# Six projection tiles of the mixing layer fed with the scaled raw stream instead of its normed form

## The reference, cut to what matters

```python
def first_block(x, c, positions, ...):
    cond = jax.nn.silu(c)
    mod = cond @ w_ada[l] + b_ada[l]
    sh1, sc1, gt1, sh2, sc2, gt2, sh3, sc3, gt3 = split(mod, 9)
    u = modulate(rmsnorm(h, g_norm_ffn1[l]), sh1, sc1)
    h = h + 0.5 * gt1 * swiglu(u, w_ffn1_in[l], w_ffn1_out[l])
    u = modulate(rmsnorm(h, g_norm_mix[l]), sh2, sc2)
    h = h + gt2 * token_mixing(u, cos, sin, w_in[l], ...)
    ...
```

## Time and profile before

| | us |
|---|---|
| median of three executions | 2532.84 (2530.0 to 2533.72) |
| the profiled execution | 2532.03 |
| its span in the trace | 2530.2 |
| TensorE busy in it | 2445.1 (97%) |
| VectorE busy in it | 1801.1 (71%) |
| ScalarE busy in it | 1106.5 (44%) |
| bytes read from memory | 451.09 MB, 179 GB/s over the span |

### The profile page before, as it was taken

The page is one execution under the profiler, slowest core; times in us unless marked ns, Lnnn a source line. Parts: engine busy times, 40 slices in busy tenths (PEclk is TensorE's granted clock), DMA queues, the critical chain, the costliest instruction groups (busy, mean ns, idle before and its releaser), DMA issues.

```text
span 2530.2 us, 39280 instructions
## 1 busy us (share of the span) xinstructions
PE 2445.1 (97%) x15654; PEld 2226.9 (88%) x15654; DVE 1801.1 (71%) x3467; ACT 1106.5 (44%) x1656; POOL 0.2 (0%) x4
## 2 busy tenths in 40 slices
PE   4998999999999999999999999999999999998998
PEld 3998989999999888788888998888998888988997
DVE  7888887788977446768877669897785344676555
ACT  3444565544463324724223662232562222566443
POOL 0000000000000000000000000000000000000000
PEclk8999999999999999999999999999999999999999
DMA  8997656769855431653543256676374333122653
GB/s 317 334 332 266 211 193 191 250 234 313 304 196 188 140 100 59 208 159 125 154 141 121 85 183 202 192 237 199 119 241 148 94 125 95 62 92 91 202 185 99
DMA packets 161671, 454.72 MB, mean 180 GB/s; under 512 B 17745, under 2 KB 21329, under 8 KB 161489
## 3 DMA queue, kind: packets, MB, share of 16 engines
q1 hardware_dynamic: 161488, 452.21, 54.3%
HBM read 451.09 MB, written 1.05 MB: 179 GB/s over the span
## 4 chain that ended last, share of the span: by engine, by line
PE 77%; DVE 4%; ACT 4%; issue 1%; DMA 0%; ACTq 0%; DVEq 0%; SPq 0%
PE PS L1297 24%; PE PS L1299 24%; PE PS L1298 24%; DVE own L1803 1%; PE PS L1457 1%; PE PS L1324 1%; PE PS L1322 1%; ACT own L1525 1%; ACT Uh L1588 1%; PE PS L1506 1%; ACT NT L1592 1%; DVE X L1784 1%; PE PS L1489 0%; DVE X L1899 0%; ACT spare L1525 0%
## 5 line engine op out<-in xcount | busy, mean ns | idle before, releaser
L1297 PE MATMUL PS<-Uh,own 128*128 128x256 f32 (+1 forms) x2080 | 655.1, 315 | 30.4 <-DVE Ul L1888 21.7
L1298 PE MATMUL PS<-Ul,own 128*128 128x256 f32 (+1 forms) x2080 | 646.6, 311 | 0.0
L1299 PE MATMUL PS<-Uh,own 128*128 128x256 f32 (+1 forms) x2080 | 646.4, 311 | 0.0
L1525 ACT ACTIVATE own<-raw 128x1024 fp32r<-128x1024 f32 x425 | 443.3, 1054 | 360.9 <-PE PS L1299 298.6
L1803 DVE TENSOR_TENSOR own<-raw,own 128x1024 fp32r<-128x1024 f32 x425 | 515.0, 1220 | 76.6 <-ACT own L1525 76.2
L1297 PEld LDWEIGHTS PS<-Uh,own 128*128 128x128 f32 x2080 | 401.5, 193 | 55.4 <-issue 29.5
L1298 PEld LDWEIGHTS PS<-Ul,own 128*128 128x128 f32 x2080 | 401.8, 193 | 19.8 <-issue 0.2
L1299 PEld LDWEIGHTS PS<-Uh,own 128*128 128x128 f32 x2080 | 401.6, 193 | 19.7
L1297 PE MATMUL PS<-Hh,own 128*128 128x256 f32 (+1 forms) x1088 | 345.2, 317 | 0.0
L1298 PE MATMUL PS<-Hl,own 128*128 128x256 f32 (+1 forms) x1088 | 340.9, 313 | 0.0
L1299 PE MATMUL PS<-Hh,own 128*128 128x256 f32 (+1 forms) x1088 | 340.9, 313 | 0.0
...
## 6 DMA issues: line engine op xcount, KB each, us to landing
...
```

The source lines that it names most:

```text
L1297: e.matmul(o, ll, rh, start=start, stop=False, skip_group_check=shared)
L1298: e.matmul(o, lh, rl, start=False, stop=False, skip_group_check=shared)
L1299: return e.matmul(o, lh, rh, start=False, stop=stop, skip_group_check=shared)
L1525: e.activation(parts(w.n)[0], raw[:, w.n % RING, :], ACT.Copy).then_inc(s["whi"].tell(w.n), 1)
```

## The change: raw operands, and sums between them

For six tiles TensorE no longer waits for the norm. The token's reciprocal is a factor per token and the shift adds a constant per output feature, so both can be applied behind the product. ScalarE and VectorE write high and low parts of `X` times gain into the columns 256 to 511 of `Uh` and `Ul` ("rawhi", "rawlo"); the shift stands in two further columns, for which the rows of both tiles grow from 512 to 528 words (`UW`). The matmuls of these tiles have 258 columns. The first stops after six rows for the sums of squares, then goes on. VectorE multiplies each result by the reciprocal, copies the product with the shift to `lift`, and ScalarE adds it. The normed rows are still made, for the tiles from the seventh on. The first four rows' squares are folded on VectorE, not the first six. Two places in `spare` are opened in the first layer, so that two more chunks are split ahead; the queries that are written over them wait for those chunks' products. The rates of mods change: 1.7 in place of 1.5 in the first layer and 0 in its last slab, 0.6 in the remaining projections (0.9 before), 0.9 for values and attention (0.9, then 0.6), 1.5 for the gates (0.9), 1.6 in the second feed-forward layer (1.4). `T2`, a tile of the second block's mixing, moves onto the first 128 columns of the bias tile in `GW`.

```diff
+UW = 528
+RAW = 6
+RAW_FOLDED = 4
...
@@ class Plan
-        if len(t["todo"]) > BEHIND:
+        if sums and len(t["todo"]) > BEHIND:
             self.sums(t)
...
+            self.raw_lows()
             for k in (mm,) if alone else (mm - 1, mm):
-                self.square(self.tallies[LAT], k)
+                self.square(self.tallies[LAT], k, RAW_FOLDED if raw else FOLDED, not raw)
+                if raw:
+                    self.put("rawhi", st=raw, k=k, after=(st, at, k, 0))
+                    self.raws.append((raw, k))
...
@@ schedule
-    p.rate = 1.5
-    main = p.ffn("w1", "w1o", LAT, [(("w1", 0), "half", 0, 2)], False)
+    p.rate = 1.7
+
+    def before_raw():
+        p.column(("nm", "c"), "gm", 0, 4)
+        p.mod_until(0, 3)
+        p.put("rawshift", q=0, f=3)
+        p.rate = 0.0
+
+    main = p.ffn("w1", "w1o", LAT, [(("w1", 0), "half", 0, 2)], False, then={len(SLABS) - 1: before_raw}, raw="nm")
...
+    for at in (0, 1):
+        p.open(at, "modded", (31, 0))
...
-    p.rate = 0.9
-    first = p.rms("nm", 0, 3, "gm", (0, 0), w1_last, 0, ("wpqk", [("wpqk", t_) for t_ in range(3)]))
...
+    p.clear = [c for at in (0, 1) for c, _, _ in p.close(at)]
+    t = p.tallies.pop(LAT)
+    raw = [p.raw_tile("wpqk", 0, 0, 6)]
+    p.raw_lows()
+    while t["todo"]:
+        p.sums(t)
+    raw[0] = p.raw_tile("wpqk", 0, 6, KT, raw[0].n, raw[0].bank)
+    p.put("stat", n=t["n"], r=LAT, bank=t["bank"], eps=1e-6)
+    raw.append(p.raw_tile("wpqk", 1, 0, KT))
+    p.put("root", n=t["n"], r=LAT)
...
+    for k in range(0, KT, 2):
+        for kk in (k, k + 1):
+            p.put("rms", st="nm", k=kk, n=t["n"], r=LAT, after=w1_last, q=0, f=3)
+        if len(made) < RAW:
+            made.append(p.raw_tile("wpqk", len(made), 0, KT))
+        raise_one()
...
+    p.rate = 0.6
...
+    p.rate = 0.9
...
-    p.rate = 0.9
+    p.rate = 1.5
...
-    p.rate, p.mod_limit = 1.4, EARLY_PAIRED * 16
+    p.rate, p.mod_limit = 1.6, EARLY_PAIRED * 16
...
@@ build
-        Uh = sb("Uh", [P, KT, 512], F32R)
-        Ul = sb("Ul", [P, KT, 512], F32R)
+        Uh = sb("Uh", [P, KT, UW], F32R)
+        Ul = sb("Ul", [P, KT, UW], F32R)
...
@@ TensorE
+                elif w.what == "rawmm":
+                    on.wait_ge(s["wlo"], w.n)
+                    if w.k == 0:
+                        claim(w.bank)
+                    for k in range(w.k, w.f):
+                        on.wait_ge(s["raw_lo"], k)
+                        m = three(PS[:, w.bank[0], 0:S + 2], *weights(w.n, k), Uh[:, k, S:2 * S + 2], Ul[:, k, S:2 * S + 2],
+                                  k == 0, k == KT - 1)
...
@@ ScalarE
+                elif w.what == "rawhi":
+                    on.wait_ge(s["acc"], w.after)
+                    on.wait_ge(s["coef"], (w.st, "c"))
+                    e.activation(Uh[:, w.k, S:2 * S], X[:, w.k, 0:S], ACT.Copy,
+                                 scale=cf((w.st, "c"))[:, w.k:w.k + 1]).then_inc(s["raw_hi"].tell(w.k), 1)
...
@@ VectorE
+                elif w.what == "rawlo":
+                    on.wait_ge(s["raw_hi"], w.k)
+                    e.scalar_tensor_tensor(out=Ul[:, w.k, S:2 * S], in0=X[:, w.k, 0:S], scalar=cf((w.st, "c"))[:, w.k:w.k + 1],
+                                           in1=Uh[:, w.k, S:2 * S].bitcast(F32), op0=ALU.mult, op1=ALU.subtract).then_inc(
+                        s["raw_lo"].tell(w.k), 1)
+                elif w.what in ("pool_in", "qk1") and w.raw:
+                    on.wait_ge(s["matmul"], w.after)
+                    on.wait_ge(s["rstd"], w.n)
...
+                        for c in plan.clear:
+                            on.wait_ge(s["matmul"], plan.used[c])
...
+                    e.tensor_copy(lift[:, w.j:w.j + 1], PS[:, b, S:S + 1])
+                    e.tensor_tensor(dst, PS[:, b, 0:S], RS[:, 0, 0, :], ALU.mult).then_inc(s["raised"].tell(w.j), 1)
```

More of the change, by code:

```diff
@@ L138 @@
     kept: bool = False
+    raw: bool = False
 class Plan:
@@ L549, in hidden_by_now, with kept_tile @@
                 f()
-    def kept_tile(self, st, c, slab, at, qs, mm, banks, first, final, norm):
+    def kept_tile(self, st, c, slab, at, qs, mm, banks, first, final, norm, raw):
         per = 8 // len(slab)
@@ L578, in out_tile, with outer @@
         return w
-    def outer(self, st, w_out, first, slab, at, qs, r, norm=None, banks=None, final=False):
+    def outer(self, st, w_out, first, slab, at, qs, r, norm=None, banks=None, final=False, raw=None):
         per = 8 // len(slab)
@@ L586, in outer @@
             if banks:
-                w = self.kept_tile(st, c, slab, at, qs, mm, banks, first == 0, final, norm)
+                w = self.kept_tile(st, c, slab, at, qs, mm, banks, first == 0, final, norm, final and raw)
             else:
@@ L618, in ffn @@
     def ffn(self, st, w_out, r, gates, norm, slabs=SLABS, base=0, width=FS, early=0, alone=0, at=0,
-            then={}, ahead=(), further=0):
+            then={}, ahead=(), further=0, raw=None):
         firsts = [sum(len(x) for x in slabs[:n]) for n in range(len(slabs))]
@@ L631, in out @@
             return self.outer(st, w_out, firsts[n], slabs[n], n + at, [slots[f] for f in slabs[n]],
-                              LAT if n < alone else r, norm, banks, n == len(slabs) - 1)
+                              LAT if n < alone else r, norm, banks, n == len(slabs) - 1, raw)
         for n, slab in enumerate(slabs):
@@ L733, in context_hidden, with raise_one @@
         yield
[L735 to L736 removed]
     p.put("padding")
[L738 to L742 removed]
+    p.norming = True
+    p.clear = [c for at in (0, 1) for c, _, _ in p.close(at)]
[8 more added lines that the diff above has]
+    p.put("root", n=t["n"], r=LAT)
+    p.release(t)
+    def raise_one():
+        i = raw.index(None)
+        w, raw[i] = made[i], 0
+        what, k = ("pool_in", i) if i < 2 else ("qk1", i - 2)
+        p.put(what, st="wpqk", n=t["n"], k=k, j=i, bank=w.bank, after=(w.id, 0), raw=True)
+    made, raw = raw, [None] * RAW
+    for k in range(0, KT, 2):
[4 more added lines that the diff above has]
+        raise_one()
+    p.put("rms", st="nm", k=KT, n=t["n"], r=LAT, after=w1_last, q=0, f=3)
+    p.norming = False
+    while None in raw:
+        raise_one()
+    p.rate = 0.6
+    pending, pooling = list(range(RAW - 2)), [0, 1, 2, 3]
     def rope_one():
@@ L1221, in build @@
         last_mix = (find("mix", f=CT - 1).id, 0)
+        last_raw = (max(w.id for w in plan.order if w.what == "rawmm"), 0)
         last_score1, last_gather1 = (find("score1", k=7).id, 2), (find("gather1", k=7).id, 0)
```

79 lines of the change are left out of this document (56 added, 23 removed).

## The result

| | before | after |
|---|---|---|
| median of 20 executions each, us | 2530.71 (2528.97 to 2534.86) | 2536.39 (2533.74 to 2538.69) |
| after / before | | 1.002, 95% interval 1.0013 to 1.0027 |
| span of the profiled execution, us | 2530.2 | 2536.6 |

The change is slower by 0.2%, 5.7 us; forecast were 2522 and a gain. Part 1 of the page after answers to the earlier trace rows: TensorE is busy 7.3 us longer, with four more records.

The account below looks back on a forecast made before the run. TensorE, busy 97% of the span, was taken as the bound, so only its idle or low-clock time could go: 2532.03 - 11.9 + 0.5 + 1.0 = 2521.6, forecast 2522 us; 8-in-10 range 2518 to 2529.

Parts of the forecast that it names:

- The end of the layer: First raw tile at the feed-forward layer's end: TensorE stalls 1.9 us in pieces for raw low parts, no low clock.
- the five other tiles: Remaining raw tiles, 14.4 us, cover the norm; normed rows arrive in time with 0.5 us to spare, so nothing lost.
- behind it: Chunks 8 to 17, after the raw tiles: low halves stay ahead except one late at the context, 0.9 us.
- Wider rows: Uh and Ul rows 528 words apart: no row shows such a pitch, so cost taken as 0.
- Rival C: Slower: moved mods come out on TensorE, up to 2542; or slower wide-row reads, 1.3 ns each cancelling 11.9; chance 0.05.
- Bounds below: Promise, at the 528-word rows, to give limits for their cost after taking it as 0.
- 7.7 and 5.6 us fit: Moved mods fit VectorE's idle time at the gates (7.7) and in attention (5.6); 0.5 us booked.
- The first layer: 9 more mods up to its last slab: bounds 0 and 6.3 us, 1.0 taken.
- rival A: First layer runs out of lead through added mods or the transfer limit: 2526 to 2530 us, chance 0.12.
- The sum: Whole kernel: 2532.03 - 11.9 + 0.5 + 1.0 = 2521.6, with the median 0.8 above, so 2522 us.
- The base: Starting time of the forecast for the whole kernel: this execution's 2532.03 us, the median shown 0.8 above it.

Follow-up runs that it names:

- e2: Kernel before with only Uh and Ul rows widened to 528 words and T2 on the bias tile: 2537.98 against 2531.57 us.
- e3: Changed kernel with rows of 512 words, the two shift columns left out: 2527.12 against 2531.57 us.
- e5: TensorE alone, no model product: rows 512 words apart, start of rows and of weights moved by some words; 226.7 to 233.4 ns a matmul at 512 columns.
- e8: Kernel before with only the change's rates of mods: 2538.32 against 2530.86 us.
- e9: Kernel before with ring chunks used with 256 columns alone begun 16 words later: 2514.32 against 2530.60 us.
- e12: Kernel before with Uh, Ul, Hh, Hl, all tiles behind them and the 512-column ring chunks moved 16 words: 2512.64 against 2531.70 us.
- e11: Changed kernel, Uh rows 576 words, ring chunks as in e9, mods 0.6 in last slab, then 0.6, 1.2, 1.5: 2514.50 against 2530.60 us.
- e13: Changed kernel with Uh rows of 576 words, mods of e11, rows and chunks moved as in e12: 2510.29 against 2531.70 us.
- e7: Changed kernel with Uh rows of 576 words, mods at 2.0 in the first layer, 0.6 in attention, 1.2 at gates: 2530.11 against 2530.86 us.

## Why the prediction was wrong

- **The end of the layer, the five other tiles, behind it: right.** Forecast 11.9 us to the pooling map, measured 12.1 in the change and 12.0 with narrow rows (from +0.6 to -11.4). Row by row the stalls at the raw rows were smaller than the 1.9 us booked (0.8 in named waits), the one for the context larger (1.4 for 0.9), so that the total fits better than its parts.
- **"Wider rows. No row shows a pitch of 528 words; taken 0": this step failed.** It cost 6.4 us alone (e2) and 10.1 in the change (change and e3, each against its own before). Rival C had the mechanism and the price at which it decides, 1.3 ns on 9,000 matmuls; it was 5.0 ns on the 3168 with 512 columns, and -1.5 on the 6720 with 256. What it had wrong was the chance: no row of before could show a row that begins elsewhere, as all of its rows begin multiples of 256 bytes apart, and so none spoke against it. "Bounds below" were promised, and none went into the range. Of the rules on the chip one spoke for zero: the Trainium skill, "TensorE: Matmul & The Clock Gate", section "Step-by-step: what each phase is for", says that the weights' load has a read port of its own and takes no read bandwidth from the running matmul. By that one would not expect the place of the weights to count, and the measurement decides: moving the weights alone by 128 bytes took a matmul from 226.7 to 232.4 ns (e5). Whether the ports are the reason, no run shows.
- **"7.7 and 5.6 us fit": this failed too.** Booked 0.5 for attention and nothing for the gates; in e3 4.4 and 1.9 us went there, in e8 4.1 and 1.8. At the end of the second layer, whose three mods were booked at nothing, 1.3 more went between 705 and 739 us in every run with 1.6 mods per chunk there, and nothing in e2, e9 and e12 with 1.4 (with 1.5, 1.3 in e11 and 2.7 in e13). The prediction asked how much of VectorE is idle over 80 us. But in e8 and e3 attention's loss lies between 345 and 355 us, where only one or two of the moved mods stand: one ahead of the rows of `X` made a wait of 0.7 us one of 1.7 to 2.1, with a low clock behind it (0.56 in e8), a price that the prediction had only at the norm. The moved mods behind that, up to 450 us, cost nothing there.
- **The first layer: right, by little.** Booked 1.0, measured nothing at 1.7; e7 shows the cliff of rival A at 2.0.
- **The sum.** -12.0 + 6.3 + 1.3 makes -4.4, which is the median of e3 (its profiled execution ends 5.0 ahead). The 10.1 for the rows are the difference from there to the change, +5.7, and so no check of it. The base was high too: 2532.84 is the median of three executions, 2530.71 that of twenty.
